# The boundary between two layers of an encoder on one core: layers written out, split activations straight from PSUM, value columns in the first projection tile

## What is computed

```
for l in range(2):
    h = rms_norm(x, ln_mix[l])
    z = h @ w_in[l]      # [c_q 384 | c_kv 256 | k_rope 32 | q_B 512 | k_B 128 | v_B 128 | g_A 1024 | g_B 1024]
    y_a = mla_attention(...)              # 8 heads
    y_b = window_attention(q_B, k_B, v_B) # 8 heads, band of 128 with a bias
    x = x + (sigmoid(g_A) * (y_a @ w_oa) + sigmoid(g_B) * (y_b @ w_ob)) @ w_out
    h = rms_norm(x, ln_ffn[l])
    # each token: 2 of 32 experts, f = 256
    x = x + sum(gate_e * ((silu(h @ w_gate[e]) * (h @ w_up[e])) @ w_down[e]))
y = rms_norm(x, ln_final)
```

## Time and profile before

| | us |
|---|---|
| Median of 3 runs (1430.33 to 1431.72) | 1431.5 |
| The profiled execution's own time | 1433.39 |
| Its span, first to last instruction | 1431.6 |
| PE busy in the span | 1265.0 |
| DVE, ACT, POOL busy in the span | 565.6, 414.6, 214.2 |

### The profile page before, as it was taken

One profiled execution on the slowest core, in us unless ns is written; L12 is line 12 of the kernel. 1 busy time (PEld: TensorE's weight loads), 2 busy tenths in 40 slices (PEclk: granted clock), 3 DMA queues, 4 the chain that ended last, 5 costly groups with the idle time before them and its releaser, 6 DMA issues.

```text
span 1431.6 us, 16922 instructions
## 1 busy us (share of the span) xinstructions
PE 1265.0 (88%) x5950; PEld 829.8 (58%) x5950; DVE 565.6 (40%) x849; ACT 414.6 (29%) x809; POOL 214.2 (15%) x212
## 2 busy tenths in 40 slices
PE   4998879999966999999869998899999479999996
PEld 3975557777753454444458655577777434445443
DVE  6245552344351233323482355434343403233334
ACT  4315662222111221211342356422221122112122
POOL 4322530000003111100040225200000031111000
PEclk8999999999986999999979999999999789999998
DMA  8503003332066999999612030043310869999971
GB/s 270 181 1 89 1 1 103 89 88 78 34 276 243 417 414 416 416 413 402 183 38 85 1 89 1 1 147 89 88 59 30 358 247 416 415 415 413 414 302 59
DMA packets 119456, 278.53 MB, mean 195 GB/s; under 512 B 12976, under 2 KB 74928, under 8 KB 102992
## 3 DMA queue, kind: packets, MB, share of 16 engines
q1 hardware_dynamic: 111824, 259.53, 48.0%
q0 software_dynamic: 6400, 13.74, 2.9%
q10 hardware_dynamic: 1152, 4.19, 0.7%
HBM read 279.51 MB, written 8.40 MB: 201 GB/s over the span
## 4 chain that ended last, share of the span: by engine, by line
PE 77%; DVE 6%; issue 6%; ACT 3%; DVEq 2%; PEldq 2%; DMA 1%; PEld 1%; POOL 1%; ACTq 0%; POOLq 0%; SPq 0%
PE bank L1125 72%; PE bank L1374 2%; PE bank L1247 1%; PEldq L1403 1%; ACT arena L719 1%; DVE arena L811 1%; DVEq L806 1%; PEld bank L1125 1%; DVE small L943 1%; DMA lns<-gains 1%; POOL arena L561 1%; DMA arena<-token_rows,idx 1%; PEldq L1426 1%; PE bank L1409 1%; ACT arena L723 1%
## 5 line engine op out<-in xcount | busy, mean ns | idle before, releaser
L1125 PE MATMUL bank<-arena 128*64 128x512 f32 (+5 forms) x1442 | 332.0, 519 | 48.0 <-DVEq L1084 14.7
L1125 PEld LDWEIGHTS bank<-arena 128*64 128x64 f32 (+2 forms) x1442 | 155.8, 157 | 199.9 <-issue 142.2
L1125 PE MATMUL bank<-ring,arena 128*64 128x512 f32 (+2 forms) x928 | 206.2, 564 | 11.0 <-issue 6.0
L1125 PEld LDWEIGHTS bank<-ring,arena 128*64 128x64 f32 (+1 forms) x928 | 81.0, 149 | 125.6 <-issue 125.4
L1125 PE MATMUL bank<-y_parts,chosen 128*128 128x512 f32 x512 | 135.0, 408 | 5.3 <-DVE y_parts L1108 4.9
L590 POOL MEMSET arena<- 128x1024 f32 x32 | 30.6, 958 | 681.7 <-DVEq L1094 451.1
L1063 DVE TENSOR_TENSOR x<-x,bank 128x512 f32<-128x512 f32 x128 | 88.0, 688 | 72.1 <-PE bank L1125 72.1
L1125 PEld LDWEIGHTS bank<-y_parts,chosen 128*128 128x128 f32 x512 | 92.1, 191 | 28.0 <-issue 8.8
L1125 PE MATMUL bank<-hT_gate_low,w_chunk_high 128*128 128x512 f32 x256 | 103.8, 406 | 3.5 <-issue 3.1
L1125 PE MATMUL bank<-hT_gate_high,w_chunk_low 128*128 128x512 f32 x256 | 102.1, 399 | 0.0
L1125 PE MATMUL bank<-hT_gate_high,w_chunk_high 128*128 128x512 f32 x256 | 101.8, 398 | 0.0
(11 more groups left out here) (200 smaller groups left out, 1881.2 us busy)
## 6 DMA issues: line engine op xcount, KB each, us to landing
ring<-w_gate SPq DMA_DIRECT2D x32, 1024.0 KB, 11.4
ring<-w_up SPq DMA_DIRECT2D x32, 1024.0 KB, 15.9
ring<-w_down SPq DMA_DIRECT2D x32, 1024.0 KB, 15.8
arena<-w_gate SPq DMA_DIRECT2D x32, 1024.0 KB, 12.0
arena<-w_up SPq DMA_DIRECT2D x32, 1024.0 KB, 17.3
arena<-w_down SPq DMA_DIRECT2D x32, 1024.0 KB, 16.2
ring<-w_in SPq DMA_DIRECT2D x36, 512.0 KB, 5.9
ring<-w_in SPq DMA_DIRECT2D x4, 1024.0 KB, 12.9
```

The source lines that it names most:

```text
L1125: return pe.matmul(out, lhsT, rhs, start=first, stop=last)
```

## The change

The two layers are written out (`for l in range(L)`), so the loop's jump at the end of layer 0 and the registers that held `l` are gone. Feature block `k` is now features 128k to 128k+127: the norms read and write without a stride, `w_in` and the router's weights are read as `(k p)`, and `w_gate` and `w_up` are put in order before the launch, so that their loads stay as they were. At a layer's start ACT writes only `hT_in[0]`, all eight halves, and DVE subtracts it from PSUM to make `hT_in[1]`; POOL adds the two to `hT` later. PE does tile 0 after the transposes of chunks 0 and 1, and transposes chunks 2 and 3 between the tiles 0, 1 and 2. The 128 value columns join tiles 0 to 3 (416 columns); tiles 13 to 16 are gone. Weight part 0 is split in layer 0 by ACT and DVE between the norms, in layer 1 by POOL while the last pair runs. Its high part lies where the band bias goes, so the bias loads wait for the end of tile 3. In the experts, the drains after `gate_up` and `down` are gone; the last product for each expert increments a semaphore itself, and `y_ps` counts halves, so ACT starts on half 0 of a result before half 1 is done. The last group's units come in another order, the first waits for three of the four low parts, and ACT loads the root's table after the last SiLU. At the kernel's start `gain` is loaded from ACT's queue, part 0 ahead of chunks 1 to 3 of `x`, and the bias product moves to tile 3. The diff, cut to its core:

```diff
-PARTS = ((D_CQ, N_TOK - D_CQ, 0), (0, D_CQ, 2304), (COL_QB, 256, 5376), (COL_QB + 256, 256, 7424), (COL_KB, 256, 9472))
+N_KV = N_TOK - D_CQ
+PARTS = ((D_CQ, N_KV + P, 0), (0, D_CQ, 3328), (COL_QB, 256, 6400), (COL_QB + 256, 256, 8448), (COL_KB, P, 10496))
-        w_in0_high_at = wq_at + 2112
+        w_in0_high_at = bias_at
-        NZ, NZ_OUT = 17, 9
+        NZ, NZ_OUT = 13, 7
+        LAST_UNITS = (0, 2, 1, 3, 4, 5, 6, 7)
 # SP
-            with sp.Fori(0, L) as l:
+            load_x(0)
+            for l in range(L):
-                w_in_l = rows(w_in).rearrange("(p k) n -> p k n", k=KD)
-                sp.wait_ge(pair_used, sp.snap(groups_before) * 2 + 1)
+                w_in_l = rows(w_in).rearrange("(k p) n -> p k n", k=KD)
+                if l > 0:
+                    sp.wait_ge(y_ps, sp.snap(groups_before) * 8)
+                sp.dma_start(in_parts[0].raw[:, :, 0:N_KV], w_in_l[:, :, D_CQ:N_TOK]).then_inc(in_in[0], 16)
+                sp.dma_start(in_parts[0].raw[:, :, N_KV:], w_in_l[:, :, COL_VB:COL_GA]).then_inc(in_in[0], 16)
+                if l == 0:
+                    for c in range(1, C):
+                        load_x(c)
-                sp.dma_start(v_raw, w_in_l[:, :, COL_VB:COL_GA]).then_inc(in_in[4], 16)
 # GpSimd
+                if l > 0:
+                    w = in_parts[0]
+                    pool.wait_ge(xs_ps, pool.snap(passes_before) * (2 * PAIRS))
+                    pool.wait_ge(in_in[0], l * 32 + 32)
+                    pool.tensor_copy(w.flat_high, w.flat).then_inc(w_in0_high, 1)
+                    pool.wait_ge(w_in0_high, l + 1)
+                    pool.tensor_tensor(w.flat_low, w.flat, w.flat_high, ALU.subtract).then_inc(w_in0_low, 1)
                 pool.wait_ge(layer_done, pool.snap(passes_before) * C + C)
                 pool.memset(kz[64:128, :, 0, :], 0.0)
                 pool.memset(kz[0:64, :, 1, :], 0.0)
-                for c in range(C):
-                    pool.wait_ge(hT_act, l * 8 + c + 1)
-                    pool.wait_ge(hT_dve, l * 8 + c + 1)
-                    pool.tensor_tensor(hT_in[1][:, :, tok], hT[:, :, tok], hT_in[0][:, :, tok], ALU.subtract).then_inc(hT_low_ready, 1)
...
+                pool.wait_ge(dense_used, l * USED + 1)
                 for h in range(H):
                     pool.dma_start(win_bias[:, h, :], band).then_inc(bias_in, 16)
+                for k in range(0, KD, 2):
+                    pool.tensor_tensor(hT[:, k:k + 2, :], hT_in[0][:, k:k + 2, :], hT_in[1][:, k:k + 2, :], ALU.add)
+                pool.drain().then_inc(hT_whole, 1)
 # ScalarE
                     norm_root(c)
-                high_part(in_parts[0], in_in[0], l * 16 + 16)
+                    if l == 0 and c == 1:
+                        act.wait_ge(in_in[0], 32)
+                        act.activation(in_parts[0].flat_high, in_parts[0].flat, ACT.Copy).then_inc(w_in0_high, 1)
                 for c in range(C):
-                    norm_copy(l * 2, c, split=True)
+                    for i in (2 * c, 2 * c + 1):
+                        act.wait_ge(hT_ps, l * 16 + i + 1)
+                        act.activation(hT_in[0][...], bank[i % 4], ACT.Copy).then_inc(hT_in_high, 1)
...
-                        act.wait_ge(gate_up_used, seen * PAIRS + (r + 2))
+                        act.wait_ge(gate_up_ps, seen * (2 * PAIRS) + (2 * r + 4))
                         act.activation(silu[:, n, :], bank[2][:, 0:F], ACT.Silu).then_inc(silu_done, 1)
+                        if r == PAIRS - 1:
+                            act.activation(spare, eps, ACT.Sqrt)
...
-                        act.wait_ge(pair_used, seen * PAIRS + (r + 3))
                         for half in range(2):
+                            act.wait_ge(y_ps, seen * (4 * PAIRS) + (4 * r + 2 * half + 6))
 # VectorE
-                if perm:
-                    src, w = (v.rearrange("p (n k) -> p k n", k=KD) for v in (src, w))
+            def norm_low(l, c):
+                for i in (2 * c, 2 * c + 1):
+                    dve.wait_ge(hT_in_high, l * 8 + i + 1)
+                    dve.tensor_tensor(hT_in[1][...], bank[i % 4], hT_in[0][...], ALU.subtract).then_inc(hT_in_low, 1)
...
                     norm_chunk(l * 2, c)
-                    if c == C - 1:
-                        low_part(l, 0, in_parts[0])
+                    if l == 0 and c == 1:
+                        dve.wait_ge(w_in0_high, 1)
+                        dve.tensor_tensor(in_parts[0].flat_low, in_parts[0].flat, in_parts[0].flat_high, ALU.subtract).then_inc(w_in0_low, 1)
                     if c >= 1:
-                        norm_evac(l * 2, c - 1, split=True)
+                        norm_low(l, c - 1)
 # TensorE
-                for c in range(C):
-                    norm_transposes(l * 2, c)
+                norm_transposes(l * 2, 0)
+                norm_transposes(l * 2, 1)
                 for t in range(NZ):
                     if t < 4:
+                        if 1 <= t < 3:
+                            norm_transposes(l * 2, t + 1)
+                        if t == 0:
+                            pe.wait_ge(w_in0_low, l + 1)
+                        pe.wait_ge(hT_in_low, l * 8 + 2 * t + 2)
-                            m = mm(b[:, 0:P], hT[:, k, c * P:(c + 1) * P], v_raw[:, k, :], k == 0, k == KD - 1)
...
-                        if u == 0:
+                        if at == 0:
                             pe.wait_ge(pick_ready, seen * PAIRS + (2 * i + 2))
+                            pe.wait_ge(y_low, seen * (2 * PAIRS) + (4 * i + 3))
+                        if u == 1:
                             pe.wait_ge(y_low, seen * (2 * PAIRS) + (4 * i + 4))
...
-                    pe.drain().then_inc(gate_up_used, 1)
+                            if k == KD - 1:
+                                m.then_inc(gate_up_ps, 1)
...
-                    pe.drain().then_inc(pair_used, 1)
+                                if f == FC - 1:
+                                    m.then_inc(y_ps, 1)
```

More of the change, by code:

```diff
@@ L612, in norm_root, with norm_copy @@
                 act.activation(root[:, c:c + 1], sumsq[:, c:c + 1], ACT.Sqrt, bias=eps, scale=1.0 / D).then_inc(root_done, 1)
-            def norm_copy(ns, c, split=False):
+            def norm_copy(ns, c):
                 tok, ps = slice(c * P, (c + 1) * P), bank[2 * c % 4][:, :].rearrange("p (k t) -> p k t", k=4)
                 act.wait_ge(hT_ps, ns * 8 + 2 * c + 1)
-                copied = act.activation(hT[:, 0:4, tok], ps, ACT.Copy)
-                if split:
-                    copied = act.activation(hT_in[0][:, 0:4, tok], ps, ACT.Copy)
-                copied.then_inc(hT_act, 1)
+                act.activation(hT[:, 0:4, tok], ps, ACT.Copy).then_inc(hT_act, 1)
+            act.dma_start(gain, gains[0:1, :].broadcast_to([P, D])).then_inc(gain_in, 16)
             act.wait_ge(const_in, 16)
-            with act.Fori(0, L) as l:
+            act.activation(spare, eps, ACT.Sqrt)
+            for l in range(L):
                 for c in range(C):
@@ L830, in step @@
                 return ins
-            dve.wait_ge(bias_ps, 1)
-            dve.wait_ge(const_bias, 48)
-            dve.tensor_tensor(makings[0:H, 1536:2048], bank[0][0:H, :], makings[0:H, 1024:1536], ALU.add).then_inc(bias_sb, 1)
             dve.wait_ge(const_in, 16)
-            with dve.Fori(0, L) as l:
+            for l in range(L):
                 dve.wait_ge(gain_in, l * 32 + 16)
@@ L1466 @@
     arrays["gains"] = np.concatenate([np.stack([inputs["ln_mix"][l], inputs["ln_ffn"][l]]) for l in range(L)] + [inputs["ln_final"][None]])
+    for n in ("w_gate", "w_up"):
+        arrays[n] = np.ascontiguousarray(arrays[n].reshape(L, NE, KD, P, F).swapaxes(2, 3)).reshape(L, NE, D, F)
     arrays |= shape_constants()
```

174 lines of the change are left out of this document (92 added, 82 removed).

## The result

The changed kernel takes 1382.5 us (median of 4 runs, 1374.13 to 1388.14) beside 1430.9 for the kernel before in the same job: a ratio of 0.9658, 95% interval 0.9606 to 0.9711. A second set gave 1387.0 (6 runs, 1376.97 to 1388.65) beside 1430.7.

The account below looks back on a forecast made before the run. PE was taken as the bound, busy 88% of the span and setting the experts' pace. The terms -17.0 - 14.6 - 5.4 + 2.2 - 2.6 - 3.4 + 0.5 gave -40.3, from 1431.5 to 1391 us; range 1379 to 1408.

Parts of the forecast that it names:

- Drains: In the experts: without the drains a pair loses 0.6 us of PE idle; 8.5 us per layer, -17.0 us.
- Value columns: In the projections: tiles 13 to 16 go, 7.3 us of PE each layer, -14.6 us.
- Boundary: From layer 0's last down to the end of layer 1's tile 3: 6.0 us earlier, -5.4 without the drains' 0.6.
- The blocked `chosen`: Last pair's selection on DVE at the layer boundary: shut out by POOL's subtraction until 706.5, costing 5 us.
- The hole of 2.93 us: On DVE at its loop end between the layers: a gap without cause, expected to be gone before the norm.
- Start: Kernel start to the end of layer 0's tile 3: ends at 45.9 instead of 43.7, +2.2 us (bounds -3 and +5).
- Second norms: Second norm of each layer: 0.8 us shorter, all counting on the last chunk, about 0.5 on the first; -2.6 us.
- the copies of k: Copies now behind the last tile: about 0.25 us twice, +0.5 us.
- The end: Last combine starts when down ends, not 2.4 us later, without the idle ahead where the clock fell: -3.4 us.
- (a): Rival at the boundary: `chosen` gets in ahead of POOL's subtraction, the 5 us are not lost, 1386 us; chance 0.28.
- (b): Rival in the experts: late loads replace the drains, PE waits, a layer gains 3 us not 8.5; 1402 us; chance 0.12.
- (d): Rival in the experts: late weights leave idle gaps that lower PE's clock, slower than before at 1456 us; chance 0.03.

## Why the prediction held, and where its terms were off

The forecast was 1391, faster; measured were 1382.5 and 1387.0, inside the range. The sum was made in one execution: it gave 1433.39 - 40.3 = 1393.1, the profiled run took 1388.1. The 5 us lie in all parts but the start.

1. **Drains**, -17.0: -17.9 by the marks, -18.2 and -16.5 when they were taken or given back alone. The total is right, its two sizes are not. "Without them a pair loses 0.6 us of idle" is 0.85, as 0.25 us of it counted as busy time. "What is late next are the weights" is right, and their price is not 0.9 us per layer but 3.5 to 4.3. The two errors nearly cancel, because the pace that the prediction read from the loads, 15.6 us, lies so close above PE's.
2. **Value columns**, -14.6: -15.0. A stretch in which PE had almost no idle time before or after gave what its rows said. No run took this part alone.
3. **Boundary**, -5.4: -6.3. The blocked `chosen` came as predicted: 7.48 us, where the working has it from 699.7 to 707.2, and 5.33 us of idle time on PE, where it took 5. Against that, "combine runs 8.09" was 9.5: behind 5.3 us of idle the clock fell to 0.83, which the prediction had counted for the end of layer 1 and not here. The sum came out because tiles 0 to 3 took 20.9 us where it had 22.2. The hole of 2.93 us was DVE's loop end. The memsets cost the norm beside them nothing (1.28 us at 703.11, POOL's at 702.64 and 703.62).
4. **Start**, +2.2: +2.2, tile 3 ending at 45.90 as worked out. The steps were right (tile 0 at 23.14 for 22.8); that the sum fits to a tenth is luck, as tile 3 ends between 45.8 and 47.0 in the eight profiles with this start.
5. **Second norms**, -2.6, and the copies of k, +0.5: together -4.2. Layer 0 gave 1.35 and layer 1 2.9, where the prediction had the same in both. A single fall of the clock in the attention is worth 1.8, so two executions alone would not settle it, but the others agree: the stretch took 357.3 to 357.7 us in the two other kernels with the old norms, in either layer, and in the nine profiles with the new ones and the drains of this stretch 356.5 to 356.9 or 358.4 to 358.7 in layer 0, 354.3 to 354.8 (in two of them 356.4) in layer 1. Between the lower values that is some 0.9 and 3.0: the term was mis-sized by about 2 us, nearly all in layer 1, and what gave them there is not shown.
6. **The end**, -3.4 "of at most -3.8": -4.1. Halves put together again cost 3.6 us there. Of the 4.1, 1.6 hang on the clock that fell in the one execution of before: before without drains and before with DVE's loop out have the same wait there, did not meet the fall, and need 27.8 and 28.0 us to the end where before needs 29.6. Against them the change gives 2.4.

Of the rivals, (a) is a question of 0.3 us, decided anew in each run as far as the times tell, and given 0.28; the selection moved out of POOL's way is worth 9.2 by the medians and 6.7 and 8.2 by the marks, not 5, since the idle time behind the lock also cost the clock. It does not make it certain: where the weights landed 1.2 us earlier, POOL's cast held the moved selection up for 2.79 us. (b) came true in part: PE does wait for `w_up`, but the layer kept 9 us of its gain and not 3. (d) did not come: gaps of 0.5 us for weights left the clock in the experts at 1.00.

## What to carry to other kernels

A drain on TensorE's queue for the sake of an increment costs more than the idle time that its row shows: put the increment on the last product, everywhere, and look at what loads that uncovers; when the transfers are already full, read their pace first, for it is the floor of the gain. Before an engine gets new work from SBUF in a stretch that another engine's short instruction decides, ask which of the two is there first, and cut the long one into pieces or put the short one ahead. A short idle time of TensorE ahead of a burst of products can be paid twice: behind 2.44 us of waiting 32 products took 1.4 us longer in four cases of eight, and behind 5.3 us 1.2 and 2.3 us longer than without a wait in the same kernel. So part of a measured gain can hang on whether the clock fell in the one execution that was read.

## What had not been expected of the hardware

Two drains per pair cost 0.85 us with 0.6 shown as idle; taking out the 23 others per layer gave about 0.3 us for each. GpSimd's instruction was held up by VectorE's as VectorE's was by GpSimd's (1.00 for 0.53 us, 7.48 for 0.69), by a cast too (2.79 for 0.69). The same 2.44 us of idle time left TensorE's clock at 1.00 in four cases and at 0.82 or 0.83 in four. The jump at the end of VectorE's hardware loop took 2.9 us.
